# Split tiles that take the low halves of x one chunk behind the high ones, and a second-half variance placed one chunk sooner

## The reference, cut to what matters

```
def layer_norm(x, g, b):
    mu = mean(x);  var = mean((x - mu)^2)
    return (x - mu) * rsqrt(var + eps) * g + b
x = layer_norm(ALPHA * x + sublayer(x), ln_g[i, k], ln_b[i, k])
next = x @ w_in          # first tiles of the next sublayer
```

## Time and profile before

| what | value |
|---|---|
| median of 3 runs | 3359.93 us |
| profiled execution, its own time | 3359.94 us |
| its span, first to last instruction | 3358.1 us |
| PE busy | 3295.4 us (98%) |
| weight loads of PE (PEld) | 2740.5 us (82%) |
| DVE, ACT, POOL busy | 1437.4, 1371.1, 1477.9 us |
| mean granted clock of TensorE | 0.997 |

### The profile page before, as it was taken

The page is one execution under the profiler, slowest core; times in us unless marked ns, Lnnn a source line. Parts: engine busy times, 40 slices in busy tenths (PEclk is TensorE's granted clock), DMA queues, the critical chain, the costliest instruction groups (busy, mean ns, idle before and its releaser), DMA issues. The chain is left out here.

```text
span 3358.1 us, 45351 instructions
## 1 busy us (share of the span) xinstructions
PE 3295.4 (98%) x16390; PEld 2740.5 (82%) x16390; DVE 1437.4 (43%) x2417; ACT 1371.1 (41%) x2193; POOL 1477.9 (44%) x1111
## 2 busy tenths in 40 slices
PE   8999999999999999999999999999999999999999
PEld 7888877888888888888788888887888888888777
DVE  3421466652204622125676322164365266235643
ACT  3322446542223522224554322256355255445553
POOL 5544433154543454443323554445454354354423
PEclk9999999999999999999999999999999999999999
DMA  4322222022222223222211222232221222232111
GB/s 168 144 96 98 88 69 69 14 94 97 97 94 88 81 100 99 95 88 82 69 39 57 99 95 94 101 123 100 76 76 63 76 76 69 76 126 88 57 57 63
DMA packets 78775, 289.12 MB, mean 86 GB/s; under 512 B 8736, under 2 KB 8864, under 8 KB 77472
## 3 DMA queue, kind: packets, MB, share of 16 engines
q1 hardware_dynamic: 76752, 275.77, 24.5%
q10 hardware_dynamic: 1872, 11.27, 0.9%
HBM read 280.72 MB, written 6.29 MB: 85 GB/s over the span
## 5 line engine op out<-in xcount | busy, mean ns | idle before, releaser
L600 POOL TENSOR_TENSOR w_lo<-raw,w_hi 128x512 fp32r<-128x512 f32 x1028 | 1382.1, 1367 | 1618.6 <-ACT w_hi L665 1618.5
L2091 PE MATMUL ps<-x_hi,w_hi 128*128 128x512 f32 x2544 | 1014.9, 399 | 1.9 <-DVE b_q L1825 1.0
L2093 PE MATMUL ps<-x_hi,w_lo 128*128 128x512 f32 x2544 | 991.5, 390 | 0.0
L2092 PE MATMUL ps<-x_lo,w_hi 128*128 128x512 f32 x2544 | 990.8, 389 | 0.0
L665 ACT ACTIVATE w_hi<-raw 128x1024 fp32r<-128x1024 f32 x514 | 541.6, 1055 | 970.8 <-PE ps L2093 495.0
L2091 PEld LDWEIGHTS ps<-x_hi,w_hi 128*128 128x128 f32 x2544 | 478.1, 188 | 108.1 <-issue 10.5
L2092 PEld LDWEIGHTS ps<-x_lo,w_hi 128*128 128x128 f32 x2544 | 478.2, 188 | 104.4 <-issue 8.4
L2093 PEld LDWEIGHTS ps<-x_hi,w_lo 128*128 128x128 f32 x2544 | 477.7, 188 | 100.9
L1390 DVE TENSOR_TENSOR T<-T,ps 128x512 f32<-128x512 f32 x66 | 45.4, 687 | 480.3 <-PE ps L2093 471.6
L620 POOL TENSOR_TENSOR square_parts<-T,square_parts 128x512 fp32r<-128x512 f32 (+1 forms) x71 | 87.7, 1236 | 240.2 <-ACT square_parts L1037 240.2
L2199 PE MATMUL ps<-h_hi,w_hi 128*128 128x512 f32 (+1 forms) x440 | 153.3, 348 | 0.0
(11 more groups left out here) (368 smaller groups left out, 5150.1 us busy)
## 6 DMA issues: line engine op xcount, KB each, us to landing
raw<-in_weights SPq DMA_DIRECT2D x514, 512.0 KB, 3.3
Y<-in_x_t SPq DMA_DIRECT2D x8, 256.0 KB, 6.0
mem_split<-norm_hi ACTq DMA_DIRECT2D x2, 1024.0 KB, 3.9
mem_split<-norm_lo ACTq DMA_DIRECT2D x2, 1024.0 KB, 5.9
mem_hi<-mem_split ACTq DMA_DIRECT2D x2, 1024.0 KB, 7.4
mem_lo<-mem_split ACTq DMA_DIRECT2D x2, 1024.0 KB, 10.9
out_t<-Y SPq DMA_DIRECT2D x8, 256.0 KB, 2.0
mem<-in_mem_t SPq DMA_DIRECT2D x1, 1024.0 KB, 11.6
```

The costliest lines, as they stand in the source:

```text
L600: ins = pool.tensor_tensor(g.wl[:, k, part], g.raw[:, k, part], g.wh[:, k, part], ALU.subtract)
L2091: mm(out, wh[:, c], xh[:, kc, :], start=kc == 0, stop=False)
L2092: mm(out, wh[:, c], xl[:, kc, :], start=False, stop=False)
L2093: ins = mm(out, wl[:, c], xh[:, kc, :], start=False, stop=kc == DC - 1)
```

## The change

On PE the low products of chunk kc - 1 now follow the high products of chunk kc, and those of chunk 7 come last; the statistics of the second half follow the low products of chunk 2 as before, which is now behind the high products of chunk 3. On ACT the square of the second mean goes from behind chunk 5 to behind chunk 4 and the deviation from behind chunk 6 to behind chunk 5. On DVE the second variance, with the centring of two chunks in it, goes from behind chunk 6 to behind chunk 5. The last three edits also hold for norm 7. No instruction is added or removed.

```diff
@@ norm of act_program @@
                     if j == 3:
                         late_part(1)
                         next_unit()
+                    if j == 4:
+                        mean_square(n, 1)
                     if j == 5:
-                        mean_square(n, 1)
-                    if j == 6:
                         deviation(n, 1, eps)
@@ norm of dve_program @@
                 if half == 0 and j == 3:
                     late_part(1)
-                if half == 0 and j == 6:
+                if half == 0 and j == 5:
                     variance(1)
@@ split_tiles of pe_program @@
         def part(half, tiles, last):
             cols = HALVES[half]
+            def low(kc):
+                pe.wait_ge(s.xlo_done, x_split(q, half, kc))
+                for t in tiles:
+                    wh, _ = weight(u0 + t)
+                    ins = mm(outs[t][:, cols], wh[:, kc * P:(kc + 1) * P], g.XL[:, kc, cols], start=False,
+                             stop=kc == DC - 1)
+                    if last and kc == DC - 1:
+                        ins.then_inc(s.unit_done, 1)
+
             for kc in range(DC):
                 pe.wait_ge(s.xhi_done, x_split(q, half, kc))
                 c = slice(kc * P, (kc + 1) * P)
                 for t in tiles:
                     wh, wl = weight(u0 + t)
                     mm(outs[t][:, cols], wh[:, c], g.XH[:, kc, cols], start=kc == 0, stop=False)
                     mm(outs[t][:, cols], wl[:, c], g.XH[:, kc, cols], start=False, stop=False)
-                pe.wait_ge(s.xlo_done, x_split(q, half, kc))
-                for t in tiles:
-                    wh, _ = weight(u0 + t)
-                    ins = mm(outs[t][:, cols], wh[:, c], g.XL[:, kc, cols], start=False, stop=kc == DC - 1)
-                    if last and kc == DC - 1:
-                        ins.then_inc(s.unit_done, 1)
-                if tiles == (0, 1) and kc == 2:
+                if kc:
+                    low(kc - 1)
+                if tiles == (0, 1) and kc == 3:
                     stats(q - 1, 1)
+            low(DC - 1)
```

## The result

The changed kernel takes 3363.8 us (median of 21 runs, 3362.0 to 3367.7) against 3359.6 us (21 runs, 3357.5 to 3360.7) on the same chips: ratio 1.0014, 95% interval 1.0008 to 1.0020. It is slower by 4.2 us, within the 0.2% that the prediction called no change, and inside its range. The profiled execution took 3365.9 us, 6.0 more than that of before; only 3 of the 21 runs are slower.

The account below looks back on a forecast made before the run. PE, busy 3295.4 of 3358.1 us, was taken as the bound, with low 7 of the first half setting each norm's cost. 4 x 0.30 + 2 x 0.22 + 0.73 + 0.35 = 2.72 us gave 3362.7 us, range 3359.0 to 3365.0.

Parts of the forecast that it names:

- Rival 1: The split hides PE's waits in six norms and high 3 in norm 3: 9.5 us faster, 3350.4; chance 0.07.
- the bound of +2.5: Upper bound if the wait for the square is 0.6 us more in four norms.
- The wait of 0.09 us for the square: In norm 0 the second variance on VectorE waits for the mean's square and starts 0.09 us late, at 384.72.
- own-write wait: On VectorE `scaled(7)`, now directly behind low 5, waits for its write: 0.22 us added, bounds 0 to 0.22 in seven norms.
- Rival 4: The wait of `scaled(7)` for low 5's write costs nothing: 1.2 us in all, 3361.1; chance 0.10.
- Norms 1 and 5: No wait for the square is added there, only the wait for low 5's write: +0.22 us each.
- The block takes 386.74 - 385.42 = 1.32 us: VectorE's variance block, moved ahead of `scaled(6)`, was taken to last 1.32 us in norm 0.
- Norm 3: Variance keeps its time behind slow statistics; low 7 moves from 1149.46 to 1150.46, the third tile's start by +0.73 us.
- rival 3: The clock does not fall in norm 3, which gains 0.5 us instead of losing 0.7: 3361.5; chance 0.12.
- Norm 7: Only ScalarE and VectorE change; PE gets to square 7 at 2278.16 instead of 2277.81: +0.35 us.
- rival 5: Later waits absorb the delays: 3359.9 us; chance 0.07.
- Rival 2: PE's waits move together and its clock falls to half level in six norms: 20 us slower, 3380; chance 0.04.

Follow-up runs that it names:

- e1: Only PE's new order, put into the kernel before; ACT and DVE as before: 3358.3 us, ratio 0.9998.
- e10: The changed kernel once more, unaltered, for a second trace: 3365.3 us, ratio 1.0019.
- e2: The changed kernel with PE's order of before, so only ACT's and DVE's order is new: 3365.4 us, ratio 1.0018.
- e5: The changed kernel with the second half's two centrings and the exponential back behind chunk 6; variance and logarithm stay ahead: 3361.6 us, ratio 1.0009.
- e3: The changed kernel with ACT's weight unit behind chunk 3 of the first half moved behind chunk 7, except in norm 7: 3361.5 us, ratio 1.0007.
- e9: The changed kernel with L1332, the maximum with 0, as a SCALAR_TENSOR_TENSOR with the same tile as both inputs: 3367.2 us, ratio 1.0025.
- e6: The changed kernel with 12 PE passes of the third tile done ahead of the wait for x_hi 6: 3354.5 us, ratio 0.9987.
- e7: The kernel before with PE's new order and 12 third-tile passes ahead of the wait for x_hi 7: 3351.5 us, ratio 0.9977.
- e4: The kernel before with ACT's weight unit moved from behind chunk 3 to behind chunk 7: 3355.2 us, ratio 0.9988.

## Why the prediction was right, and where it was not

**The place was right.** Low 7 of the first half ends the stretch: the third tile starts 0.87 to 0.88 us behind low 7's start in every norm where the clock holds, before and after. So PE's new order could not gain. Rival 1 fell for the second of the reasons given against it, that low 7 ends the stretch whatever precedes it: in e1 `scaled(6)` stays ahead of the block, and still nothing is gained.

**Luck in the number.** The range ended at 3365.0, below its own bounds (the forecast of 3362.7 with the bound of +2.5 alone is 3365.2). The first comparison gives 3363.8. The ten further runs of the same kernel (e10) have a median of 3365.3, just outside. The two don't contradict each other, but that the measured time lies inside owes something to which runs were taken: the four norms cost twice what the sum gave them, and norm 3 and the stretch between norms 6 and 7 gave some of it back.

**Confirmed by their sizes.** The variance in norm 0 stands 8.12 us behind `scaled(0)`, as forecast (384.72, with `scaled(0)` at 376.60). The wait of 0.09 us for the square is there (8.12 against e2's 8.03). So is the own-write wait: 387.15 - 386.54 = 0.61 us, and 0.22 gone in e5. Rival 4 went by the Trainium skill, "VectorE: DVE Perf Modes", section "The DRAIN you can't avoid", by which such a semaphore costs nothing extra. Here the measurement decides: in this chain the instruction that waits for its neighbour's semaphore starts 0.22 us later. Norms 1 and 5 cost 0.22 by the forecast and 0.23 measured at low 7. PE reaches the third tile 0.88 us behind low 7, where 0.9 was forecast.

**The mis-sized term: "The block takes 386.74 - 385.42 = 1.32 us".** In the new place it takes 1.68 in norm 0, as L1332 takes 0.64 where it took 0.30. So norms 0, 2, 4 and 6 cost 0.66 to 0.67 each at low 7, not 0.30. The prediction read POOL only for what would reach it ("POOL and SP follow it, with idle time on both"), not for what it would be doing at the block's new time. The block moved across the end of POOL's w_lo, 385.68 in the kernel before. The rows had a sign of it: the prediction put the block at 1.32 us in norm 0 and at 1.55 in norm 7 and left the difference unexplained. In norm 7 POOL works until 2276.04, and L1332 was held in the kernel before already (timelines of DVE and POOL, kernel before):

```profile
2275.69 0.50 DVE L1332 TENSOR_SCALAR T<-T 128x256 f32<-128x256 f32 x1
...
2273.54 2.50 POOL L600 TENSOR_TENSOR w_lo<-raw,w_hi 128x512 fp32r<-128x512 f32 x2 [3.99 <-ACT w_hi L665]
```

In every norm of every profile in which the TENSOR_SCALAR is long, it ends 0.15 us behind POOL. e3, which moves only the unit, brings the duration back to 0.29 and low 7 to 11.92, next to the 11.89 that the forecast makes it. With 4 x 0.35 more, the sum is 2.7 + 1.4 = 4.1 us; the medians differ by 4.2 in the first comparison and by 6.2 in e10's. That 4.1 meets 4.2 so closely is in part chance, as norm 3, norm 7, the stretch before norm 7 and the clock moved too, both ways.

**Norm 3** costs less than forecast: low 7 +0.66 instead of +1.00, third tile +0.40 instead of +0.73. The reason for the difference is the variance, which starts 0.34 us sooner behind `scaled(0)` (12.91 to 12.57), as PE is at the lower level for a shorter time. So part of rival 3 came true. **Norm 7** has the same mis-sized term: L1332 takes 0.85 where the block of before held 0.50 of it, and the memory unit starts 15.00 - 14.36 = 0.64 us later where 0.35 was forecast; 0.4 us of that is left at the end of the span. The stretch between norms 6 and 7 got 0.9 us shorter (in e10's profile 0.6), of which 0.58 is PE's wait for `ple_lo` that is gone. It is rival 5's kind of absorption, in one place; where the rest comes from is open.

**The clock.** Rival 2 was given 0.04 and 20 us. Its mechanism is real, but smaller and not steady: besides norm 3 it is three of seven norms in the first profile, two in e10's, norm 4 alone in e2's, norms 2 and 5 in e9's, none of 0, 2, 4 and 6 in e3's and e5's. In norms 0, 2, 4 and 6 a fall costs 0.5 to 0.9 us until the third tile (13.72 against 13.14 in the first profile, 14.12 against 13.27 in e9's) and 0.9 to 1.15 by the last split pass (25.50 to 25.69 against 24.54); in norm 1 of e10 0.4 (25.08 against 24.71), in norm 5 of e9 0.2. In norms 0, 2, 4 and 6 it fell behind a single idle time of 1.35 to 1.64 us. In norm 1 of e10 and norm 5 of e9 it fell behind two shorter ones (0.73 and 0.70 us, 0.87 and 0.70). Both kinds left the clock alone in other norms and executions.

The prediction said that single idle times under 1.5 us leave the clock alone, and that the trace had one such fall behind one such wait. It overlooked another in the kernel before. Behind the 1.50 us ahead of norm 7's last products the memory unit starts at the lower level (windows of the kernel before):

```profile
2278.00:2281.60 3.60, 3.60 (x10) 2.79 (x10) 3.56 (x11) 3.57 (x11) 0.00 (x0) 0.53 0.21 83
```

So the idle times that the clock can fall behind were nearer to those of the change than the 3.8 us of norm 3. The idle times of 1.12 us that rows 3 show had no fall behind them, there or in e1. The first profile has 1.03 + 1.15 + 0.98 = 3.2 us of it (25.57, 25.69 and 25.52 less 24.54) and stands 2.1 us above the median of the runs; how many falls the other runs had, their profiles would have to tell. e6, which fills the idle time, has none of it in norms 0, 2, 4 and 6; its one profile agrees with the idle time as the cause but can't prove it, as e10's profile keeps the full level in three of these norms without a fill. The Trainium skill ("TensorE: Matmul & The Clock Gate", "What's actually happening") ties the lower level to idle time, and in this the runs agree. Why the same program falls in one norm and not in its twin, and in the next execution the other way round, stays open.

## What to carry to other kernels

Before you reorder an engine that waits, find the last instant that its stretch hangs on: here it was low 7, and only work that didn't need it (the third tile's passes, 6 to 7 us) or less work ahead of it (the weight unit, 4.2 us) made a difference. Before you move an instruction on VectorE, read what GpSimd does at its new time: a TENSOR_SCALAR of 0.30 us became one of 0.64 with nothing in its own chain changed. And take an idle time of 1.4 us on TensorE, or several of 0.7 us in a row, as a risk to its clock as well, even where the norm at hand shows no fall: look through the whole trace for one behind an idle time of that size.

## What the runs showed of the hardware that I had not expected

- VectorE's TENSOR_SCALAR (128x256, SBUF to SBUF) takes 0.29 to 0.30 us alone and 0.50 to 0.86 when it starts beside GpSimd's TENSOR_TENSOR of 128x512, and then ends 0.15 us behind it; a SCALAR_TENSOR_TENSOR with two inputs in SBUF takes 0.42 and 0.86 to 0.98. Those with an input in PSUM kept their 0.42.
- VectorE's `scaled(7)` directly behind low 5, whose write it waits for, starts 0.61 us behind it, against 0.39 between neighbours that don't wait.
- TensorE's granted clock went to the 1.2 GHz level behind idle times of 1.35 to 1.64 us, or two of 0.7 to 0.87, in some executions of one program and in others not, at a cost of 0.2 to 1.15 us each (norm 2 of the first profile: a mean of 0.57 over 3.80 us).
- Whether a filled idle time makes the runs steadier stays open: e6 spreads over 1.9 us (11 runs) against the changed kernel's 5.6 (21 runs) and 4.3 (10 runs), but e7, filled too, over 4.2, and e4, not filled, over 2.05.
